# Larger and fewer weight transfers for a mixture of experts: up and down matrices of 4 MB in one transfer each, the last expert in 1 MB pieces, and TensorE reading its moving columns at a stride

## The reference, cut to what matters

```python
logits = (t @ router_w + router_b).astype(jnp.float32)
top_vals, top_idx = lax.top_k(logits, TOP_K)
...
for e in range(N_EXPERTS):
    gt = jnp.minimum(t @ exp_w_gate[e] + exp_b_gate[e], SWIGLU_LIMIT)
    up = jnp.clip(t @ exp_w_up[e] + exp_b_up[e], -SWIGLU_LIMIT, SWIGLU_LIMIT)
    act = gt * jax.nn.sigmoid(SWIGLU_ALPHA * gt) * (up + 1.0)
    out = out + combine[:, e:e + 1] * (act @ exp_w_down[e] + exp_b_down[e]).astype(jnp.float32)
```

## Time and profile before

| what | value |
|---|---|
| median of 3 runs | 1213.97 us (1212.2 to 1214.23) |
| the profiled execution's own time | 1206.91 us |
| its span, first to last instruction | 1205.2 us |
| mean granted TensorE clock | 0.993 of full speed |
| TensorE busy (PE) | 1166.7 us, 97% of the span |
| weight loads of TensorE (PEld) | 478.7 us, 40% |
| VectorE, ScalarE, GpSimd busy | 405.7, 182.4, 74.3 us |
| DMA | 456.05 MB in 53,662 packets, mean 378 GB/s |

### The profile page before, as it was taken

How to read it: one execution, slowest core, us unless ns; L and a number is a source line. 1 busy time by engine, 2 the same in 40 slices (tenths; PEclk the granted TensorE clock), 3 DMA queues, 4 the chain that set the end, 5 groups by cost and what they waited for, 6 DMA issues and landing times.

```text
span 1205.2 us, 16544 instructions
## 1 busy us (share of the span) xinstructions
PE 1166.7 (97%) x6133; PEld 478.7 (40%) x6133; DVE 405.7 (34%) x894; ACT 182.4 (15%) x305; POOL 74.3 (6%) x83
## 2 busy tenths in 40 slices
PE   8999999999999999999999999999999999999993
PEld 5676665533333333333333333333333333333331
DVE  3497225632222322232222222222223222222227
ACT  2101301211111111111111111111111111111112
POOL 4069200200000000000000000000000000000000
PEclk9999999999999999999999999999999999999997
DMA  9968664589999999999999699999999999999992
GB/s 345 373 240 305 235 245 157 201 324 417 430 427 429 429 429 428 429 429 429 428 429 402 258 404 431 427 428 427 431 428 428 427 430 428 429 427 430 429 429 88
DMA packets 53662, 456.05 MB, mean 378 GB/s; under 512 B 5321, under 2 KB 20229, under 8 KB 27019
## 3 DMA queue, kind: packets, MB, share of 16 engines
q1 hardware_dynamic: 51392, 452.87, 90.9%
q10 hardware_dynamic: 2251, 2.93, 0.8%
HBM read 454.38 MB, written 1.40 MB: 378 GB/s over the span
## 4 chain that ended last, share of the span: by engine, by line
PE 75%; DMA 19%; DVE 2%; ACT 1%; SPq 1%; issue 1%; DVEq 0%; POOLq 0%
PE bank L1590 45%; DMA ring<-in_exp_w_gate 18%; PE bank L1358 5%; PE bank L1624 5%; PE bank L1307 4%; PE bank L1541 4%; PE bank L1461 2%; PE bank L1580 2%; PE bank L1549 1%; PE bank L1445 1%; DMA ring<-in_w_ada 1%; PE bank L1277 1%; ACT arena L739 1%; PE bank L1611 1%; SPq L416 1%; PE bank L1555 1%
## 5 line engine op out<-in xcount | busy, mean ns | idle before, releaser
L1590 PE MATMUL bank<-ring,arena 128*64 128x512 f32 x3168 | 704.2, 596 | 9.5 <-POOLq L555 8.4
L1590 PEld LDWEIGHTS bank<-ring,arena 128*64 128x64 f32 x3168 | 221.9, 137 | 447.9 <-issue 406.2
L1120 DVE TENSOR_SCALAR arena<-bank 128x512 f32<-128x512 f32 x33 | 22.8, 692 | 355.3 <-PE bank L1590 355.3
L1105 DVE TENSOR_TENSOR arena<-arena,bank 128x512 f32<-128x512 f32 x132 | 84.8, 684 | 108.2 <-PE bank L1624 77.6
L739 ACT ACTIVATE arena<-bank 128x512 f32<-128x512 f32 x33 | 19.7, 597 | 375.2 <-PE bank L1555 375.2
L1624 PE MATMUL bank<-arena 64*128 64x512 f32 x264 | 74.5, 641 | 0.2 <-DVE arena L1101 0.2
L1541 PE MATMUL bank<-h,arena 128*64 128x512 f32 x272 | 64.4, 593 | 0.2 <-DVE arena L994 0.2
L1358 PE MATMUL bank<-arena,ring 128*128 128x288 f32 x256 | 63.9, 408 | 0.0
L868 DVE SCALAR_TENSOR_TENSOR h<-h,dwc 128x318 f32<-128x318 f32 x120 | 55.6, 574 | 0.0
L1358 PEld LDWEIGHTS bank<-arena,ring 128*128 128x128 f32 x256 | 48.2, 190 | 14.7 <-issue 1.7
L737 ACT ACTIVATE arena<-arena 128x512 f32<-128x512 f32 x33 | 20.8, 630 | 198.7 <-DVE arena L1120 198.7
(11 more groups left out here) (304 smaller groups left out, 737.1 us busy)
## 6 DMA issues: line engine op xcount, KB each, us to landing
ring<-in_exp_w_down SPq DMA_DIRECT2D x64, 2048.0 KB, 18.1
ring<-in_exp_w_gate SPq DMA_DIRECT2D x64, 2048.0 KB, 19.7
ring<-in_exp_w_up SPq DMA_DIRECT2D x64, 2048.0 KB, 20.4
ring<-in_w_ada SPq DMA_DIRECT2D x24, 1024.0 KB, 10.1
ring<-in_gate_w SPq DMA_DIRECT2D x8, 1024.0 KB, 7.5
ring<-in_w_in SPq DMA_DIRECT2D x6, 1024.0 KB, 19.0
ring<-in_w_out SPq DMA_DIRECT2D x4, 1024.0 KB, 6.3
ring<-in_conv_w_out SPq DMA_DIRECT2D x2, 1024.0 KB, 7.9
```

The lines of the kernel that those rows point to most:

```text
L1105: ins = v.tensor_tensor(acc[:, t, cs], acc[:, t, cs], bank[6 + hh][:, :], ALU.add)
L1590: ins = mm(out[64 * hh:64 * hh + 64, :], lhs(k), ring[:, s, D * (k % 2) + HALF * hh:D * (k % 2) + HALF * (hh + 1)], start=(done is y_mm an ...
```

## The change

Up and down matrices are loaded in one transfer of 4 MB each (4 slots, 32 KB contiguous for each partition); the gate matrix stays in two transfers of 2 MB with 16 KB runs. The first expert is still loaded in six pieces of 2 MB, and the last one in twelve pieces of 1 MB with 8 KB runs. For this a partition now holds eight neighbouring rows of each matrix, rows 8p to 8p+7, whatever the piece. To make the activations come out in the order in which down's rows now lie, the gate and up products, the gather and the bias rows take for `hh` not a contiguous half of the columns but alternate groups of four (`half_order`): four floats are read, four are skipped. The down product still reads contiguous halves. GpSimd raises `weights_ready` by the number of slots of a piece and has the last expert's loads written out behind its loop.

```diff
--- before.py
+++ after.py
@@ -55,6 +55,9 @@
 RING = 12
 SLOT = 2 * D
 PIECES = 12
+FIRST_PIECES = [(i, 2) for i in range(0, PIECES, 2)]
+MID_PIECES = [(0, 2), (2, 2), (4, 4), (8, 4)]
+LAST_PIECES = [(i, 1) for i in range(PIECES)]
 
 FRONT = ([("scale", 0, j) for j in range(4)] + [("in", c, 0) for c in (4, 2)]
          + [("shift", 0, j) for j in range(4)] + [("in", c, 0) for c in (5, 3, 0, 1)]
@@ -351,14 +354,15 @@
         poolw_v = pool_w[0].rearrange("g c o -> c g o")
         convw_v = conv_w_out[0].rearrange("(k p) n -> p k n", p=P)
         wout_v = w_out[0].rearrange("(k p) n -> p k n", p=P)
-        rows_of = "e (h p r) n -> e p h (r n)"
-        wg_v = exp_w_gate[0].rearrange(rows_of, h=2, r=4)
-        wu_v = exp_w_up[0].rearrange(rows_of, h=2, r=4)
-        wd_v = exp_w_down[0].rearrange(rows_of, h=2, r=4)
+        expert_w = [w[0].rearrange("e (p r) n -> e p (r n)", r=KD) for w in (exp_w_gate, exp_w_up, exp_w_down)]
 
         def row_order(ap, j):
 
             return ap.rearrange("p (q j) -> p q j", j=4)[:, :, j]
+
+        def half_order(ap, hh):
+
+            return ap.rearrange("p (q a j) -> p q a j", a=2, j=4)[:, :, hh, :]
 
         def front_piece(f):
 
@@ -415,23 +419,26 @@
                 src, dst = front_piece(f)
                 sp.dma_start(dst, src).then_inc(slot_ld[f % RING], 16)
 
-            def expert(e, last_use, pieces=range(0, PIECES, 2)):
-
-                for i in pieces:
-                    sp.wait_ge(piece_used, last_use(i + 1))
-                    w = (wg_v, wu_v, wd_v)[i // 4]
-                    sp.dma_start(ring[:, i:i + 2, :].rearrange("p s n -> p (s n)"), w[e][:, i % 4 // 2, :]).then_inc(slot_ld[i], 16)
+            def expert(e, last_use, pieces):
+
+                for i, k in pieces:
+                    sp.wait_ge(piece_used, last_use(i + k - 1))
+                    at = SLOT * (i % 4)
+                    sp.dma_start(ring[:, i:i + k, :].rearrange("p s n -> p (s n)"),
+                                 expert_w[i // 4][e][:, at:at + SLOT * k]).then_inc(slot_ld[i], 16)
 
             def front_use(i):
                 return max(f for f in range(N_FRONT) if f % RING in (i, i + 1)) + 1
 
             for i in sorted(range(0, PIECES, 2), key=front_use):
-                expert(0, lambda _: front_use(i), (i,))
+                expert(0, lambda _: front_use(i), [(i, 2)])
             sp.wait_ge(base_ready, 1)
-            with sp.Fori(1, E) as e:
+            with sp.Fori(1, E - 1) as e:
 
                 at = sp.value_load(base_i[0:1, bass.ds(e, 1)], min_val=1, max_val=MAX_ITEMS)
-                expert(e, lambda i: at * PIECES + (F_END - PIECES + i + 1))
+                expert(e, lambda i: at * PIECES + (F_END - PIECES + i + 1), MID_PIECES)
+            at = sp.value_load(base_i[0:1, E - 1:E], min_val=E - 1, max_val=MAX_ITEMS)
+            expert(E - 1, lambda i: at * PIECES + (F_END - PIECES + i + 1), LAST_PIECES)
             at = sp.value_load(base_i[0:1, E:E + 1], min_val=E, max_val=MAX_ITEMS)
             sp.wait_ge(piece_used, at * PIECES + (F_END - PIECES + 1))
             sp.wait_ge(rows_out[1], 64)
@@ -546,13 +553,22 @@
                 pool.wait_ge(slot_ld[i], (USES[i] + 1) * 16)
                 pool.sem_inc(weights_ready, 2)
             pool.wait_ge(base_ready, 1)
-            items = pool.value_load(base_i[0:1, E:E + 1], min_val=E, max_val=MAX_ITEMS)
+            last_first = pool.value_load(base_i[0:1, E - 1:E], min_val=E - 1, max_val=MAX_ITEMS)
             pool.wait_ge(owner_ready, 1)
-            with pool.Fori(1, items) as n_i:
-                e = pool.value_load(owner_i[0:1, bass.ds(n_i, 1)], min_val=0, max_val=E - 1)
-                for i in range(0, PIECES, 2):
+            with pool.Fori(1, last_first) as n_i:
+                e = pool.value_load(owner_i[0:1, bass.ds(n_i, 1)], min_val=0, max_val=E - 2)
+                for i, k in MID_PIECES:
                     pool.wait_ge(slot_ld[i], (e + (USES[i] + 1)) * 16)
-                    pool.sem_inc(weights_ready, 2)
+                    pool.sem_inc(weights_ready, k)
+            def loads(i):
+
+                return USES[i] + ((i, 2) in FIRST_PIECES) + (E - 2) * (i in [j for j, _ in MID_PIECES]) + 1
+
+            for i, k in LAST_PIECES:
+                pool.wait_ge(slot_ld[i], 16 * loads(i))
+                pool.sem_inc(weights_ready, k)
+            for _ in range(MAX_ITEMS_E - 1):
+                pool.sem_inc(weights_ready, PIECES)
 
 
         @block.scalar
@@ -1538,21 +1554,21 @@
 
             def gather_tile(t, start, stop=False):
                 for hh in range(2):
-                    ins = mm(bank[0][64 * hh:64 * hh + 64, :], oh[:, t, :], h2[:, t, HALF * hh:HALF * (hh + 1)],
+                    ins = mm(bank[0][64 * hh:64 * hh + 64, :], oh[:, t, :], half_order(h2[:, t, :], hh),
                              start=start, stop=stop, skip_group_check=True)
                 return ins
 
             def gather_strips(lookup, start=False, stop=True):
 
                 for hh in range(2):
-                    out, cs = slice(64 * hh, 64 * hh + 64), slice(HALF * hh, HALF * (hh + 1))
-                    mm(bank[3][out, :], mine[B_GATE, :], bias_rows[B_GATE, cs], start=True, stop=False, skip_group_check=True)
-                    mm(bank[4][out, :], mine[B_UP, :], bias_rows[B_UP, cs], start=True, stop=False, skip_group_check=True)
+                    out = slice(64 * hh, 64 * hh + 64)
+                    mm(bank[3][out, :], mine[B_GATE, :], half_order(bias_rows[B_GATE, :], hh), start=True, stop=False, skip_group_check=True)
+                    mm(bank[4][out, :], mine[B_UP, :], half_order(bias_rows[B_UP, :], hh), start=True, stop=False, skip_group_check=True)
                     if lookup:
                         for i in range(2):
                             found = mm(bank[6 + i][out, 0:TOK], mine[LOOKUP, :], routedT[:, i, :], start=True, stop=True,
                                        skip_group_check=True)
-                    ins = mm(bank[0][out, :], oh[0:NS_TOK, 2, :], h2[0:NS_TOK, 2, cs], start=start, stop=stop, skip_group_check=True)
+                    ins = mm(bank[0][out, :], oh[0:NS_TOK, 2, :], half_order(h2[0:NS_TOK, 2, :], hh), start=start, stop=stop, skip_group_check=True)
                 if lookup:
                     found.then_inc(lookup_mm, 1)
                 return ins
@@ -1580,6 +1596,10 @@
                     ins = tr(bank[1][:, P * j:P * (j + 1)], row_order(xg, j), ident[:, :])
                 ins.then_inc(xgT_mm, 1)
 
+            def weights(s, k, hh, done):
+                rows_ = ring[:, s, D * (k % 2):D * (k % 2 + 1)]
+                return rows_[:, HALF * hh:HALF * (hh + 1)] if done is y_mm else half_order(rows_, hh)
+
             def product(out, lhs, n_i, c0, done, mid=None, before_used=None):
 
                 for k in range(KD):
@@ -1588,7 +1608,7 @@
                         pe.wait_ge(weights_ready, n_i * PIECES + (s + 1))
                     for hh in range(2):
                         ins = mm(out[64 * hh:64 * hh + 64, :], lhs(k),
-                                 ring[:, s, D * (k % 2) + HALF * hh:D * (k % 2) + HALF * (hh + 1)],
+                                 weights(s, k, hh, done),
                                  start=(done is y_mm and k == 0), stop=(done is y_mm and k == KD - 1) or k == KD - 1,
                                  skip_group_check=True)
                         if k == 0 and hh == 0 and before_used:
```

## The result

| | before | changed |
|---|---|---|
| median in this comparison, 5 runs each, us | 1212.2 (1211.17 to 1214.23) | 1219.7 (1218.37 to 1220.19) |
| ratio of the two, 95% interval | | 1.0056 [1.0041, 1.007] |
| profiled execution, its span | 1206.91, 1205.2 | 1220.17, 1218.5 |
| granted clock | 0.993 | 0.99 |

The changed kernel is slower by 0.56%, 6.8 us, by the ratio, which is not the quotient of the two medians; these lie 7.5 us apart. The time is inside the forecast range. The two profiled executions lie 13.3 apart, and not all of that is the change: 6.25 us stand ahead of the experts. So I compare from item 0 on.

The account below looks back on a forecast made before the run. Transfers (29.37 us an item) and TensorE (28.22) were taken as close limits, with restarts and the last landing setting the end. Late events +16.4 less rate 7.3 gave +9.1 us: 1223, 8-in-10 range 1214 to 1232.

Parts of the forecast that it names:

- Term 1: Start of expert 1: up must wait for its fourth slot, so the last down transfer lands later, +4.2 us.
- Term 2: After the doubled expert: the same late issue of up and down as at expert 1, +4.2 us.
- Term 3: Doubled expert: TensorE waits for the whole of up, so it enters and frees slots later, +4.6 us.
- Term 4: End of the kernel: the last up product starts 11.0 us before the last landing instead of 14.4, +3.4 us.
- Term 5: Steady queue: fewer packets at 14.5 ns each save 0.26 us an expert over 28 experts, -7.3 us.
- The rest at nothing: Semaphores on SP and GpSimd, and products reading four floats and skipping four: no cost, zero us.
- no saving: Rival: longer runs bring no faster rate in the queue; +16.4 us, 1230; 18%.
- near the ceiling: Rival: transfer rate gains 0.50 to 0.67 us an expert, giving no difference, 1212 to 1216; 11%.
- faster: Rival: long runs in the steady queue beat the fit, from a period of 28.70; at 28.5, -8 us, 1206; 7%.
- longer steps: Rival: 32 KB steps between the streams in HBM cost rate, 8.2 us per cent; 1239 at 1% slower; 8%.
- the stride: Rival: strided columns slow TensorE to 32.2 us an item or more, about +120 us, 1336; 4%.

Follow-up runs that it names:

- e2: e1 with SP issuing both halves of up and down only when the matrix's fourth slot is free; 1218.63 us, 1.0048 of the kernel before.
- e9: e1 with 4 MB up and down transfers for experts 2, 3, 16 and 17 alone; 1217.58 us, 1.0047 of the kernel before.
- e3: e1 with GpSimd announcing up and down only when both halves have landed; 1218.84 us, 1.0053 of the kernel before.
- e1: Changed kernel with every matrix again in two 2 MB transfers, last expert too; new row order and stride stay; 1211.72 us, 0.9991 of the kernel before.
- e4: Changed kernel's transfers, but in 16 KB runs with old row order and contiguous moving columns; 1223.4 us, 1.0091 of the kernel before.
- e7: e6 with the gate rows loaded before expert 1 into other memory; 1207.53 us, 0.996 of the kernel before.
- e12: Changed kernel with the gate rows loaded before expert 1 into other memory; 1219.71 us, 1.0062 of the kernel before.
- e6: e1 with only the last expert in twelve 1 MB transfers; 1211.96 us, 0.9995 of the kernel before.
- e11: Changed kernel with the gate matrix in one 4 MB transfer too; 1219.76 us, 1.0058 of the kernel before.

## Why the prediction was right, and where it was not

The time came inside the forecast range, by the mechanism forecast: +6.8 us for +9.1, 1219.7 for 1223. Of the 3.3 us between the two times 1.8 are the base, as the sum was put on a median of 1213.97 and the kernel before has 1212.2 in this comparison. The bound stretch set in at item 5, not 7, and the waits for weights sum to 18.8 us, as said (18.5). By its own terms:

- **Term 1 (+4.2) and Term 2 (+4.2)** held: late issue alone costs 3.9 and 4.0 (e2). The hole between gate and up is 3.8, about 4 as said. What e9 adds is that with an earlier expert 1 the same price waits at expert 2.
- **Term 3 (+4.6)** held: late landing alone brings item 14 later by 4.9 (e3), and the hole at the doubled expert grew by 4.6 us (13.1 to 17.7).
- **Term 4 (+3.4)** was not isolated. From item 14 to the last the changed kernel takes 1191.19 - 672.49 = 518.70, e1 513.28: +5.42. Take off Term 2 (4.0) and add what the rate gives there (15 x 0.155 = 2.3), and 3.7 are left for it.
- **Term 5 (-7.3)** was mis-sized. The mechanism is right (e4: packets, not transfers), the price is not: 0.155 us an expert for 0.26, so 28 x 0.155 = 4.3. I had fitted 14.5 ns to a stretch of 1 KB runs whose share of the engines sums to 1.08; a sum above 1 must count some time twice, and the fit seems to have put that surplus on the packets. Two stretches and two unknowns also can't miss, so that the fit missed neither was no test of it. The runs with 16 against 32 KB give 9.4. By an estimate with 9.5 ns in both stretches, b is 36.9 us and the second stretch would have a share of 1.004 for 1.080. The bound period was said to be 29.11 and is 29.215.
- **The rest at nothing** held for stride and layout (e1).
- **Not seen at all:** the gate rows at the end. Their wait of 2.64 us was in the trace of before, and I took Term 4 for a full loss, while the first 2.6 us of any delay there fall into this wait. e7 and e12 show it from both sides: the rows early are worth 4.4 us with halves (1211.96 to 1207.53) and nothing with the change.

The measured terms are then 3.9 + 4.0 + 4.9 + 3.7 - 4.3 = 12.2. One half of this is a check: up to item 14 they say 3.9 + 4.9 - 13 x 0.155 = 6.8, and there the changed kernel is 404.40 - 397.63 = 6.8 us behind e1. The other half is none, as Term 4 was taken from what is left over in it. With the rows out of the way on both sides the difference reaches the time: e12 less e7 is 1219.71 - 1207.53 = 12.2. That it agrees to the tenth is luck. The six runs of e7 spread over 6.2 us, and e7 differs from e1 in its small last pieces and in the rows loaded ahead of expert 1, though its path from item 0 to the last is about that of e1 (911.08 for 910.91).

Against the kernel before, the row wait takes off 2.6, which leaves 9.6, and 6.8 were measured (7.5 by the medians). Some of the 2.8 is e1's: at an equal rate and with equal pieces its path from item 0 to the last item is 910.91 where before has 913.37, 2.5 us less. But its median is only 0.5 below. Part are executions that differ: after the doubled expert the kernel before is bound from item 25 on, e1 from 27 and e6, with the new row order too, from 26. Whether the row order is worth anything stays open.

The two errors, 3.0 us too much saved by the rate and 2.6 too much lost at the end, went opposite ways. The sum is better than its terms, and that is luck.

Of the rivals, "no saving" and "near the ceiling" are both excluded by the period of 29.215, as is "faster"; the costs of longer steps and of the stride are excluded by e1. By the ceiling of 435.2 GB/s in the Trainium skill ("DMA: Bandwidth & Descriptors", section "Where 436 GB/s comes from") no run length would have made up for the late events; the fastest rate in any run here is 12.583 MB in 29.14 us, 431.8 GB/s (e11), which agrees with such a limit and doesn't reach it. The rival "near the ceiling" lay beyond it: 0.50 to 0.67 us off 29.37 are 435.9 to 438.4 GB/s. The saving I had not thought of is in none of the rivals: it is the rows at the end, 4.4 us for two small transfers.

## What to carry to other kernels

In a ring without a second buffer, a piece costs its size twice: it is issued when its last slot is free and announced when its last byte has landed. Both are hidden only when queue and lead are each deeper than a piece, so look at the restarts, where the queue is empty, and at the end, before counting what a larger transfer saves. And ask what small load is queued behind the big ones before the kernel's last step: it can hide a loss, or a gain, as long as the wait for it.

## What the runs showed of the hardware

- A packet in a saturated queue costs about 9.5 ns of its engine's time, between runs of 16 and 32 KB: 428.4 GB/s with 54 packets an expert and engine, 430.7 with 36, 431.8 with 27.
- TensorE reads float32 moving columns in groups of four with four skipped at no cost: the item takes 28.22 us either way. The transposes' stationary loads that take one float in four were 208 ns long and contiguous ones of the same shape 146; no run isolates the stride there.
- The same program's front part differs between executions. Windows of 10 us (granted clock third from the right), first the kernel before, then the changed one, whose front part is the same:

```profile
110.00:120.00 10.00, 10.00 (x53) 5.81 (x52) 3.15 (x4) 0.94 (x2) 8.79 (x17) 1.00 0.91 336
```

```profile
110.00:120.00 10.00, 7.67 (x38) 3.69 (x37) 7.16 (x16) 0.50 (x1) 0.00 (x0) 0.82 0.90 342
120.00:130.00 10.00, 10.00 (x36) 7.44 (x34) 1.69 (x4) 2.20 (x3) 0.00 (x0) 0.84 0.26 105
```

TensorE was idle for 2.3 us there, and 0.82 and 0.84 are means over stretches in which part ran at the lower of its two levels (1.2 of 2.4 GHz). In the profiled execution of before it wasn't idle and stayed at 1.00. All twelve experiments have the 2.3 us of idle time, and eleven a dip of the clock behind it; e6 stayed at 1.00 and has item 0's copy at 265.02. So idle time and dip account for part of the 6.25 us that the two traces differ ahead of item 0. They look like a property of the execution and not of the change, whose front part is the same, but the kernel before was traced only once, in one of its fastest executions (1206.91 us; the others took 1207.44 to 1214.91).
